# Sixteen column blocks of an input projection computed in the recurrent preparation of a hybrid block

## What is computed

```python
proj = x @ w_in[i]                        # 2048 -> 11264 columns
sb_q, sb_k, sb_v, rw_r, rw_k, rw_v, rw_c, gate_a, gate_b = jnp.split(proj, IN_SPLITS, axis=-1)
y_a = _stick_breaking_attention(sb_q, sb_k, sb_v) @ w_up_a[i]
y_b = _rwkv7_time_mix(rw_r, rw_k, rw_v, rw_c, ...) @ w_up_b[i]
mixed = (jax.nn.sigmoid(gate_a) * y_a + jax.nn.sigmoid(gate_b) * y_b) @ w_o[i]
x = _layer_norm(DEEPNORM_ALPHA * x + mixed, ln1_w[i], ln1_b[i])
ffn = _peer_ffn(x, ..., expert_u, expert_v)
```

## Time and profile before

| | |
|---|---|
| median of 3 runs | 4803.2 us (4802.48 to 4808.9) |
| span of the profiled execution | 4800.8 us |
| mean granted clock of TensorE | 0.944 |
| PE busy | 4281.0 us, 89% |
| DVE busy | 3343.0 us, 70% |
| ACT busy | 1550.3 us, 32% |
| DMA | 1198.7 MB, mean 250 GB/s |

### The profile page before, as it was taken

One profiled execution on the slowest core, in us unless ns is written; L12 is line 12 of the kernel. 1 busy time (PEld: TensorE's weight loads), 2 busy tenths in 40 slices (PEclk: granted clock), 3 DMA queues, 4 the chain that ended last, 5 costly groups with the idle time before them and its releaser, 6 DMA issues. The chain is left out here.

```text
span 4800.8 us, 61731 instructions
## 1 busy us (share of the span) xinstructions
PE 4281.0 (89%) x23132; PEld 3809.1 (79%) x23132; DVE 3343.0 (70%) x4893; ACT 1550.3 (32%) x2737; POOL 662.1 (14%) x533
## 2 busy tenths in 40 slices
PE   8999997657888588969996699999999999999994
PEld 6888886235666567858775599999999999999994
DVE  4444443776992443449927588888888888899997
ACT  2121211343432232122226433333333333333332
POOL 0000000002441000013361011111111111111110
PEclk9999999767989889979999899999999999999997
DMA  9999998347435444964544889999999999999984
GB/s 284 311 318 309 315 311 256 113 148 150 149 114 154 153 167 145 297 212 151 161 166 120 259 308 317 312 316 321 315 315 317 318 318 316 319 315 311 317 308 184
DMA packets 588614, 1198.71 MB, mean 250 GB/s; under 512 B 69576, under 2 KB 333616, under 8 KB 531536
## 3 DMA queue, kind: packets, MB, share of 16 engines
q1 hardware_dynamic: 525248, 849.39, 57.5%
q0 software_dynamic: 46080, 335.56, 19.0%
q10 hardware_dynamic: 17040, 10.49, 0.8%
HBM read 1009.07 MB, written 228.15 MB: 258 GB/s over the span
## 5 line engine op out<-in xcount | busy, mean ns | idle before, releaser
L102 PE MATMUL h_ps<-xs,h_ut 128*128 128x352 f32 x6144 | 1077.0, 324 | 37.3 <-DVE h_ut L96 37.3
L102 PE MATMUL h_ps<-h_a,h_v 128*128 128x352 f32 x6144 | 1078.4, 324 | 12.1 <-DVE yt L2394 6.3
L102 PEld LDWEIGHTS h_ps<-xs,h_ut 128*128 128x128 f32 x6144 | 1009.7, 188 | 37.8 <-DVE h_ut L96 37.8
L102 PEld LDWEIGHTS h_ps<-h_a,h_v 128*128 128x128 f32 x6144 | 1006.3, 189 | 17.1 <-issue 7.9
L102 PE MATMUL a_ps<-xt_hi,a_w 128*128 128x512 f32 x2304 | 710.8, 390 | 8.0 <-DVE a_w L96 8.0
L102 PEld LDWEIGHTS a_ps<-xt_hi,a_w 128*128 128x128 f32 x2304 | 433.3, 188 | 98.5 <-issue 8.2
L102 PE MATMUL a_ps<-xt_lo,a_w 128*128 128x512 f32 x1152 | 448.8, 390 | 0.0
L96 DVE TENSOR_TENSOR h_v<-h_v_raw,h_v 128x512 fp32r<-128x512 f32 x512 | 351.4, 686 | 79.2 <-ACT h_v L95 78.8
L95 ACT ACTIVATE h_v<-h_v_raw 128x512 fp32r<-128x512 f32 x512 | 318.8, 623 | 240.7 <-PE h_ps L102 240.6
L96 DVE TENSOR_TENSOR h_ut<-h_u_raw,h_ut 128x512 fp32r<-128x512 f32 x352 | 242.5, 690 | 148.1 <-ACT h_ut L95 148.1
L2409 DVE SCALAR_TENSOR_TENSOR y_first<-h_rows,h_acts,y_first 128x2048 f32<-128x2048 f32 x128 | 300.4, 2347 | 0.0
(11 more groups left out here) (343 smaller groups left out, 6379.7 us busy)
## 6 DMA issues: line engine op xcount, KB each, us to landing
h_v_raw<-in_peer_v SPq DMA_DIRECT2D x128, 1024.0 KB, 8.7
h_u_raw<-turned_d SPq DMA_DIRECT2D x176, 512.0 KB, 9.3
a_raw<-in_w_in SPq DMA_DIRECT2D x36, 2048.0 KB, 12.1
a_xin<-in_peer_u SPq DMA_DIRECT2D x288, 256.0 KB, 7.6
turned_d<-a_xin SPq DMA_DIRECT2D x72, 1024.0 KB, 6.8
raw_d<-in_peer_u SPq DMA_DIRECT2D x320, 128.0 KB, 3.4
h_u_raw<-raw_d SPq DMA_DIRECT2D x80, 512.0 KB, 8.9
yt_last<-sums_d SPq DMA_DIRECT2D x125, 176.0 KB, 5.0
```

The costliest lines, as they stand in the source:

```text
L102: mm = pe.matmul(out, lhs[a], rhs[b], start=(first and n == 0), stop=(last and n == 2))
```

## The change

The input projection computes 56 blocks, and turns 56 blocks of expert rows. Column blocks 56 to 71, the first half of the two gates' columns, are computed in `rwkv_prepare` in 64 pieces, by a class `Late` that now serves attention too (there unchanged: two raw buffers, three pairs of halves). In the preparation it has three raw buffers and four pairs of halves, its loads and stores are issued from POOL's queue, and it uses PSUM banks 6 and 7. The chunk products, which had banks 4 to 7, are made in two halves in banks 4 and 5, the second after VectorE has masked the first. Four pieces stand ahead of the lora part, four behind it, and seven in each turn: two after the gate matmuls, two after the square sum, two after the bonus sum, one at the end. To make room, `b_sw`, `b_nrm` and `b_tmp` become other names of `b_lw`, `b_sq` and `b_bon`, and `b_x`, `b_gm` and `b_bkt` share one tile, `b_wide`; VectorE now waits for the store of the last bonus before the bonus product. SP copies 16 more blocks of expert rows to `raw_d` in the preparation, 16 DMAs a turn. `TURNED` falls from 88 to 72, so 16 more steps of the expert stage turn their block.

```diff
-EARLY = IN_COLS // P - LATE
+EARLY = IN_COLS // P - 2 * LATE
 TURNED = EARLY + 16
-MOVED = 22
+MOVED_BESIDE_RWKV = 16
+MOVED = 38
...
+class Late:
...
+    KQ, Q = 4, KT // 4
+    def __init__(self, sb, sem, w_in, proj_t, xt, banks, first, blocks, loads, halves):
+        self.xt, self.banks, self.first, self.blocks = xt, banks, first, blocks
+        self.pieces, self.RR, self.WR = blocks * self.Q, loads, halves
+        self.raw = [sb(f"raw{r}", [P, self.KQ, P]) for r in range(self.RR)]
+        self.half = [[sb(f"half{h}{r}", [P, self.KQ, P], F32R) for r in range(self.WR)] for h in range(2)]
+        self.ob = sb("ob", [P, T])
...
+    def load(self, queue, i):
+        if i >= self.RR:
+            queue.wait_ge(self.lo, i - self.RR + 1)
+        queue.dma_start(self.raw[i % self.RR][:, :, :], self.wv[self.first + i // self.Q, i % self.Q])\
+             .then_inc(self.raw_in[i % self.RR], 16)
+    def store(self, queue, n):
+        queue.wait_ge(self.kept, n + 1)
+        queue.dma_start(self.pv[self.first + n], self.ob[:, :]).then_inc(self.stored, 16)
+    def finish(self, queue):
+        queue.wait_ge(self.stored, 16 * self.blocks)
+    def upper(self, act, i):
+        act.wait_ge(self.raw_in[i % self.RR], 16 * (i // self.RR + 1))
+        if i >= self.WR:
+            act.wait_ge(self.used, i - self.WR + 1)
+        act.activation(self.half[0][i % self.WR][:, :, :], self.raw[i % self.RR][:, :, :], ACT.Copy).then_inc(self.hi, 1)
+    def lower(self, dve, i):
+        dve.wait_ge(self.raw_in[i % self.RR], 16 * (i // self.RR + 1))
+        if i >= self.WR:
+            dve.wait_ge(self.used, i - self.WR + 1)
+        dve.wait_ge(self.hi, i + 1)
+        dve.tensor_tensor(self.half[1][i % self.WR][:, :, :], self.raw[i % self.RR][:, :, :],
+                          self.half[0][i % self.WR][:, :, :].bitcast(F32), ALU.subtract).then_inc(self.lo, 1)
+        if i % self.Q == self.WR - 1 and i >= self.Q:
+            self.keep(dve, i // self.Q - 1)
+    def keep(self, dve, n):
+        dve.wait_ge(self.used, self.Q * n + self.Q)
+        if n >= 1:
+            dve.wait_ge(self.stored, 16 * n)
+        dve.tensor_copy(self.ob[:, :], self.banks[n % 2]).then_inc(self.kept, 1)
+    def multiply(self, pe, i):
+        n, q = divmod(i, self.Q)
+        pe.wait_ge(self.lo, i + 1)
+        if q == 0 and n >= 2:
+            pe.wait_ge(self.kept, n - 1)
+        for k in range(self.KQ):
+            d = self.KQ * q + k
+            mm = product(pe, self.banks[n % 2], [self.half[h][i % self.WR][:, k, :] for h in range(2)],
+                         [z[:, d, :] for z in self.xt], d == 0, d == KT - 1)
+        mm.then_inc(self.used, 1)
 L = 64
 NC = T // L
...
         e_in, e_out, e_prev = (sb(n, [P, T]) for n in ("e_in", "e_out", "e_prev"))
-        kk, sq, nrm, k2, tmp, bon = (sb(n, [P, T]) for n in ("kk", "sq", "nrm", "k2", "tmp", "bon"))
+        kk, sq, k2, bon = (sb(n, [P, T]) for n in ("kk", "sq", "k2", "bon"))
+        sw, nrm, tmp = lw, sq, bon
         gs = sb("gs", [P, T])
         ar = sb("ar", [P, NC, 2, L])
...
-        bkt = sb("bkt", [P, NC, P])
+        wide = sb("wide", [P, 6, T])
+        x3 = wide[:, :, :].rearrange("p (u j) t -> p u j t", u=2)
+        gm = wide[:, 0:4, :].rearrange("p b t -> p (b t)").rearrange("p (c e j) -> p c e j", c=NC, e=2)
+        bkt = wide[:, 4:6, :].rearrange("p b t -> p (b t)").rearrange("p (c j) -> p c j", c=NC)
...
+        late = Late(sb, sem, w_in, proj_t, xt, [ps[:, 6 + n, :] for n in range(2)], EARLY, LATE, 3, 4)
+        u_moved = sem("u_moved")
+        FIRST = 4
+        AFTER = {"lora": 4, "gate": 2, "square": 2, "bonus": 2, "turned": 1}
+        PER_HEADS = sum(AFTER.values()) - AFTER["lora"]
+        assert FIRST + AFTER["lora"] + MB * PER_HEADS == late.pieces
+        def pieces_of(m, name):
+            names = ["gate", "square", "bonus", "turned"]
+            i = FIRST + AFTER["lora"] + m * PER_HEADS + sum(AFTER[n] for n in names[:names.index(name)])
+            return range(i, i + AFTER[name])
...
+            for i in range(late.pieces):
+                late.load(pool, i)
+                if i % late.Q == 0 and i >= 2 * late.Q:
+                    late.store(pool, i // late.Q - 2)
+            late.store(pool, LATE - 2)
+            late.store(pool, LATE - 1)
+            late.finish(pool)
...
+                for h in range(2 * MOVED_BESIDE_RWKV // MB):
+                    move_u(sp, expert_u, raw_d, 2 * MOVED_BESIDE_RWKV // MB * m + h, u_moved)
...
+            pe.transpose(ps[:, 4, 0:NV * MB], rows[:, :], ident[0:NV * MB, 0:NV * MB]).then_inc(s["pe"], 1)
+            for i in range(FIRST):
+                late.multiply(pe, i)
...
+            for i in range(FIRST, FIRST + AFTER["lora"]):
+                late.multiply(pe, i)
             pe.wait_ge(s["act"], AC1)
+            def chunks(m, half):
+                for ch in range(4 * half, 4 * half + 4):
+                    for e in range(2):
+                        q = slice(64 * e, 64 * e + 64)
+                        j = ch % 4
+                        mm = pe.matmul(ps[:, 4 + e, j * P:(j + 1) * P],
+                                       bk[q, ch, :, :].rearrange("p a l -> p (a l)"),
+                                       ar[q, ch, :, :].rearrange("p a l -> p (a l)"), start=True, stop=True)
+                mm.then_inc(s["pe"], 1)
+            def pieces(m, name):
+                for i in pieces_of(m, name):
+                    late.multiply(pe, i)
             for m in range(MB):
...
+                pieces(m, "gate")
                 pe.wait_ge(s["act"], ac_.at(m, "square"))
                 pe.matmul(ps[:, 3, :], ones[:, :], sq[:, :], start=True, stop=True).then_inc(s["pe"], 1)
+                pieces(m, "square")
                 pe.wait_ge(s["act"], ac_.at(m, "norm"))
                 pe.wait_ge(s["dve"], dv_.at(m, "rk_part"))
                 pe.matmul(ps[:, 3, :], ones[:, :], tmp[:, :], start=True, stop=True).then_inc(s["pe"], 1)
+                pieces(m, "bonus")
                 pe.wait_ge(s["dve"], dv_.at(m, "bonus"))
...
-                for ch in range(NC):
-                    for e in range(2):
-                        q = slice(64 * e, 64 * e + 64)
-                        j = ch % 4
-                        mm = pe.matmul(ps[:, 4 + 2 * e + ch // 4, j * P:(j + 1) * P],
-                                       bk[q, ch, :, :].rearrange("p a l -> p (a l)"),
-                                       ar[q, ch, :, :].rearrange("p a l -> p (a l)"), start=True, stop=True)
-                mm.then_inc(s["pe"], 1)
+                chunks(m, 0)
...
+                pe.wait_ge(s["dve"], dv_.at(m, "masked1"))
+                chunks(m, 1)
+                pieces(m, "turned")
...
+            for i in range(FIRST + AFTER["lora"]):
+                late.upper(act, i)
             act.wait_ge(s["pe"], p1pe.at(MB - 1, "lora"))
...
+                pieces(m, "gate")
                 act.wait_ge(s["pe"], pe_.at(m, "decay_in"))
...
+                pieces(m, "square")
                 act.wait_ge(s["pe"], pe_.at(m, "square_sum"))
...
+                pieces(m, "bonus", "turned")
                 act.wait_ge(s["pe"], pe_.at(m, "bk_turned"))
...
+            for i in range(FIRST):
+                late.lower(dve, i)
...
+            for i in range(FIRST, FIRST + AFTER["lora"]):
+                late.lower(dve, i)
...
+                pieces(m, "gate")
                 dve.wait_ge(s["act"], ac_.at(m, "log_decay"))
...
+                pieces(m, "square")
                 dve.wait_ge(s["act"], ac_.at(m, "norm"))
...
+                if m >= 1:
+                    dve.wait_ge(s["st_bon"], 16 * m)
                 c.then("rk_part", dve.scalar_tensor_tensor(tmp[:, :], r[:, :], par(10, m), k2[:, :],
...
+                pieces(m, "bonus")
                 dve.wait_ge(s["act"], ac_.at(m, "e_prev"))
...
-                    dve.wait_ge(s["st_bon"], 16 * m)
...
-                dve.wait_ge(s["pe"], pe_.at(m, "chunks"))
+                pieces(m, "turned")
...
+                for half in range(2):
+                    dve.wait_ge(s["pe"], pe_.at(m, f"chunks{half}"))
+                    for e in range(2):
+                        c.mark(f"masked{2 * half + e}", dve.tensor_tensor(
+                            gm[:, 4 * half:4 * half + 4, e, :],
+                            ps[:, 4 + e, :].rearrange("p (a j) -> p a j", j=2 * L),
+                            mask[:, :, :].rearrange("p a l -> p (a l)").unsqueeze(1).broadcast_to([P, 4, 2 * L]),
+                            ALU.mult))
+            late.keep(dve, LATE - 1)
...
+                if i - RR < 2 * (MOVED - MOVED_BESIDE_RWKV):
+                    move_u(sp, expert_u, raw_d, 2 * MOVED_BESIDE_RWKV + i - RR, u_moved)
```

109 lines of the change are left out of this document (35 added, 74 removed).

## The result

The changed kernel takes **4727.5 us** (median of 4 runs, 4725.3 to 4732.6) beside 4802.8 us for the kernel before: ratio 0.9846, 95% interval 0.9832 to 0.9860. Timed again (run 8) it took 4727.9 beside 4798.9 us, 0.9846 again (0.9828 to 0.9863). The forecast was 4717 us, with a range of 4693 to 4763. Direction and size came out; 10.5 us are left to explain, and they hide a fault that was worth more: 17.9 us over the eight turns (run 5).

A forecast was written before the change was run, and what follows sets the result against it. TensorE was taken to bound the input projection and expert stage, the preparation to be a chain between engines. -174.0 + 69.3 + 10 - 1 + 9.5 = -86.2 from 4800.8 gave 4714.6, with 2.4 for the median 4717 us; range 4693 to 4763.

The forecast's parts named there:

- First stage: Input projection: 16 of 72 blocks removed, each 48 matmuls of 226.5 ns, all on the path, -174.0 us.
- Lead-in: Preparation before its first turn: eight added pieces, first load ready after 5 us, +10 us, bounds 5 and 18.
- The best turn: A preparation turn with nothing late: 29.1 us of PE work plus about 1.5 us idle, 30.6 us.
- Turns of 32.5 us by late loads and clock: Eight preparation turns: best turn plus 1.1 us for loads and 0.8 for clock each, +69.3 us in all.
- (b): Rival: POOL queue's loads take 8.1 us each and the clock falls in every preparation turn, 4748 us; 20%.
- Clock: Preparation turns: TensorE idle of 1.5 to 2.5 us costs 1.6 us of half clock in half of them, 0.8 each.
- (a): Rival: nothing is late in the preparation, turns of 30.6 us, -15 us, 4702 us; 25%.
- (c): Rival: the preparation's clock does not rise; 4827 us at 0.65, 3%; near 0.69 nothing changes, 2%.
- (d): Rival: the expert steps pay their added block turning in full, 45.2 us instead of 9.5, 4753 us; 3%.
- (e): Rival: DMA is the bound in the preparation turns, some 4770 us; 2%.
- Experts: Expert stage: 16 more steps turn their block, 16 groups of four pay 0.6 us each, +9.5 us.
- Attention: Attention stage: costed at nothing; a change in its length would show the forecast wrong.

The follow-up runs named there:

- run 8: The changed kernel timed again with no edit: 4727.9 us, beside 4798.9 us for the kernel before.
- run 5: Changed kernel with four raw buffers instead of three and each block store issued two loads later, behind load 4n+10: 4707.1 us.
- run 6: Run 5 with one of the two pieces ahead of the sum of squares moved behind it, three pieces ahead of the root: 4696.4 us.
- run 11: Changed kernel with its three raw buffers and each block store issued two loads later, behind load 4n+10: 4712.7 us.
- run 9: Changed kernel with the turning of 16 blocks left out of the expert stage, which reads 16 other, already turned blocks: 4718.8 us.
- run 2: Changed kernel with the copies of 16 expert blocks moved from the preparation to the attention stage: 4743.0 us.
- run 1: Changed kernel with each block store issued one load later, behind load 4n+9: 4719.6 us.
- run 10: Run 5 with both pieces ahead of the sum of squares moved behind it, four pieces ahead of the root: 4726.7 us.
- run 4: Changed kernel with four raw buffers instead of three, queue order unchanged: 4721.3 us.

## Why the prediction was right, and where it was not

- **First stage, -174.0 us**: measured -173.9, at the same 226.5 ns. Right.
- **Lead-in, +10**: measured +11.0. The first loads landed 5.9, 9.1, 10.7 and 8.7 us after their issue, later than the 5 us assumed and three of them later than the 8.1 of the upper bound. But the first three are issued together, and TensorE went from the first piece to the fourth with one gap of 0.39 us: the four took 13.4 us (662.73 to 676.16) where the forecast had 13.6. Right, with a price of a load that was too low and did not bind.
- **The best turn, 30.6 us**: the parts were 29.1 us of PE and 1.5 of idle. Run 5 shows 240.29 / 8 = 30.0 us of PE and 1.16 us of idle, 31.2 together. The idle time was rounded up: the forecast's own times, 17.2 less 16.0, give 1.2. The chunk products, which had no row at full clock, are 1.16 us for each half, 2.3 and not the 1.9 I took of bounds 1.9 to 3.8 (two lines of run 6, TensorE):

```profile
772.04 1.16 PE L555 MATMUL b_ps<-b_ar,b_bk 64*128 64x128 f32 x16
...
775.03 1.16 PE L555 MATMUL b_ps<-b_ar,b_bk 64*128 64x128 f32 x16
```

- **Turns of 32.5 us by late loads and clock**: the sum was +69.3 and is +76.7, and this is the step that failed. I wrote of the tight piece that "its load may start at t = 3.7" because its buffer was free there, and gave every turn the same 1.1 us for a slower landing. I had costed the store as a DMA beside the others, and had not asked what is queued behind its wait. In turn 1 the load was issued in a row of three that began at t = 4.7, and rounded at t = 12.2. That turn has 4.9 us over turn 0: 2.3 us more idle before the bonus sum, 0.8 us before a piece, and 1.8 us more of PE busy by the clock. The order of the queue stands in the diff, and the pattern of turns 1, 2, 5 and 6 could have been worked out from it beforehand.
- **Luck in the size.** The 1.9 us a turn for loads and clock make 15.2 us over eight turns; measured are 17.9 over run 5, which has no late piece. But they lie in four turns of 3.8 to 4.9 us each and not in eight of 1.9, and come from a wait that the forecast did not have. The mean of 33.4 us is near the forecast's 32.5 by luck. Three signs on record say so: turn 1 passes 36 us (36.1), TensorE is idle ahead of pieces too (0.8 us in turn 1), and it is ScalarE's split that waits for the load, up to 8.2 us, which was the sign of (b). The "5.7 us" of room for a landing let the root's table load run ahead; in a late turn its 1.28 us stand behind the rounding. Runs 11 and 5 say that three buffers are just short, by 3.9 us over all eight turns.
- **Clock**: the size held. The changed kernel's quick turns stay at 1.00, and its four others, with 2.59 to 4.01 us of idle time, lose some 1.7 us each to half clock, as I had from the earlier trace rows: 246.86 less 240.29 us of PE in run 5 are 6.6 over the eight turns, where the forecast had 8 x 0.8 = 6.4. That a half of the turns would pay it was forecast; which ones, and that late loads would be the reason, was not.
- **Rival (b)**, late loads with the clock falling, 4748 us at 20%: its mechanism is what happens in four turns of eight, by the queue and not by the POOL path's speed. That is, the loads are late and the clock falls, but landings had 5.2 us in the median and not 8.1. Its turn, 3.9 us over the forecast's 32.5, would be 36.4 us; turns 1, 2, 5 and 6 take 35.6 in the mean. **Rival (a)**, nothing late, 4702 us, is run 5, which takes 4707.1 us with its turns at 31.2 and a lead-in of 68.0 us, not the 66.4 of the forecast. (c), (d) and (e) did not come: the clock rose to 0.97, the expert groups paid 0.6 us, and run 6 carries a DMA share of 0.77 with TensorE never idle.
- **End, -1**: it is +0.7. The last store is issued at 987.1 us and the next stage begins 8.5 us later; I had let it land beside the others.
- **Experts, +9.5**: measured +8.0 between the two kernels' products (2033.6 to 2041.6 us), and -9.7 in run 9. The rows of one group, 62.10 and 62.60 above, stand beside the 62.02 and 62.61 worked out from the earlier trace rows.
- **Attention, 0**: it got 3.2 us longer, which I had named as a sign against the forecast. Its code did not change, and in the twelve profiles that leave it so (the changed kernel, and all runs but 2) it takes 426.6 us (run 11) to 434.0 (run 1), with the 429.9 of the kernel before among them. The 3.2 us are within this scatter, and I should have written down its width rather than a sign. What makes it scatter by 7 us was not tried.

The 10.5 us over the forecast are 7.4 for the turns (4.7 by the best turn, 31.2 for 30.6, and 2.7 by what is late), 1.0 for the lead-in, 1.7 for the end, 3.2 for attention and 0.9 for the other stages and rounding, less 1.8 for the experts and 1.9 for the distance from span to median.

## What to carry to other kernels

A store in a queue of loads is a wait for everything behind it: put it behind every load whose buffer is free before the store's data is, and write the queue's order down against the pieces' deadlines, turn by turn, since a period of 4 against one of 7 makes some turns late and others not. Where one repair brings little, look for a second bound on the same path before you drop it: the fourth buffer was worth 1.2 us, which one profile does not tell from nothing, then 3.9, then 10.1 as the bounds beside it went, and the third piece ahead of the root turned from a loss of 3.8 us into a gain of 11.0. Work that is moved into a chain's holes pays by which hole it lies in: the longest one is to be covered first, and only as much may stand ahead of it as the chain's other engines are ready for (run 10). A piece that stands in front of the start of a chain delays the chain; behind its start it covers it: moving one such piece brought the root from 10.8 to 8.0 us into the turn (run 6).

## What the runs showed of the hardware

**Short idle times of TensorE and its clock.** In the turns of the thirteen profiles (the changed kernel and runs 1 to 12) I listed TensorE's idle times over 0.7 us and whether a stretch at half clock begins in the idle time or within 1.3 us of its end:

| idle time, us | how many | with half clock |
|---|---|---|
| up to 1.82 | 61 | 0 |
| 2.03 to 2.26 | 15 | 10 |
| 2.34 to 3.19 | 14 | 11 |
| 3.41 to 4.08 | 19 | 19 |

Between 2 and 3.2 us the same idle time is followed by either level. One that was not, the 3.19 us in turn 1 of run 4, and the stretch behind it at full clock:

```profile
769.82 1.10 PE L577 MATMUL b_ps<-b_bon,b_ones 128*128 128x512 f32 x2 [3.19 <-DVE b_bon L710]
```
```profile
769.80:773.20 3.40, 3.38 (x13) 2.47 (x14) 3.40 (x6) 0.00 (x0) 1.90 (x3) 1.00 0.20 78
```

So in these turns a hole of up to 1.8 us cost itself, and a longer one up to nearly twice what it was longer: from 1.16 to 3.94 us of idle a turn went from 31.2 to 36.6.

**A load from GpSimd's queue.** The issue of 256 KB takes GpSimd 0.75 us, and the landing, counted from the start of the issue, 3.2 us at least, 4.0 in the median where no block copies run beside it (run 2) and 5.0 to 6.1 where they do. The Trainium skill, "DMA: Bandwidth & Descriptors", section on the anatomy of one DMA on the gpsimd path, gave 2.6 us, an estimate by its formula; no landing of such a load in any run is as short. Of the blocking of that path by VectorE, of which "SBUF — State Buffer" of the Trainium skill speaks in its section on the two separate sides, the issues show nothing: 747 ns at least, 749 in the median and 962 at most with VectorE busy in 189.5 of 267.4 us. The page ties it to VectorE's two-port mode, and no trace here shows which instructions ran in it, so this does not speak against the page.
